# Two stages of a one-core transformer kernel: own buffers for the first slots behind the experts, another order of sums there, and other PSUM banks in block 1

## The reference

```python
# first block
proj = rms_norm(x, norm_mix) @ w_in             # qa ka va | qd kd vd | gates
out_na = neighbourhood_attention(qa, ka, va)    # 8 heads of 64
out_dil = dilated attention, 3 groups of 4 heads, softmax over all three groups
merged = sigmoid(gate_na) * (out_na @ w_branch_na) + sigmoid(gate_dil) * (out_dil @ w_branch_dil)
x = x + merged @ w_out
x = x + peer_ffn(rms_norm(x, norm_ffn))         # 16384 experts, 8 heads, top 16 each
h = rms_norm(x, norm_ple)
x = x + sigmoid(h @ w_ple_gate) * (p @ w_ple)
# second block: attention, pooling, feed forward, final norm
```

## Time and profile before

| | |
|---|---|
| time, median of 3 runs | 1334.89 us (1333.16 to 1335.21) |
| time of the profiled execution | 1334.01 us |
| its span, first to last instruction | 1331.8 us |
| TensorE busy | 1307.1 us (98%) |
| VectorE busy | 1018.5 us (76%) |
| ScalarE busy | 827.0 us (62%) |
| GpSimd busy | 513.2 us (39%) |
| mean granted TensorE clock | 0.994 of full speed |

### The profile page before, as it was taken

The page is one execution under the profiler, slowest core; times in us unless marked ns, Lnnn a source line. Parts: engine busy times, 40 slices in busy tenths (PEclk is TensorE's granted clock), DMA queues, the critical chain, the costliest instruction groups (busy, mean ns, idle before and its releaser), DMA issues.

```text
span 1331.8 us, 24822 instructions
## 1 busy us (share of the span) xinstructions
PE 1307.1 (98%) x9818; PEld 1261.1 (95%) x9818; DVE 1018.5 (76%) x1849; ACT 827.0 (62%) x1679; POOL 513.2 (39%) x248
## 2 busy tenths in 40 slices
PE   9999899999999999999999999999998999999997
PEld 9999799999999999999989999999998999999997
DVE  4573545759999888899978798998867855899943
ACT  6563556545455888888755565555565766666652
POOL 4745566578901000000024444434201553794442
PEclk9999999999999999999999999999998999999999
DMA  8433345555656555545569999999863544556552
GB/s 307 143 111 111 112 130 185 166 174 175 193 189 202 194 173 161 170 162 173 160 236 327 355 340 335 331 337 324 291 210 124 175 130 140 181 172 193 186 188 96
DMA packets 74299, 268.36 MB, mean 201 GB/s; under 512 B 8252, under 2 KB 8636, under 8 KB 74184
## 3 DMA queue, kind: packets, MB, share of 16 engines
q1 hardware_dynamic: 64968, 233.22, 52.7%
q0 software_dynamic: 9216, 33.56, 6.8%
HBM read 265.70 MB, written 1.05 MB: 200 GB/s over the span
## 4 chain that ended last, share of the span: by engine, by line
PE 81%; DVE 10%; POOL 3%; ACT 2%; DMA 1%; issue 1%; SPq 0%; DVEq 0%; ACTq 0%
PE PS L601 81%; POOL SPL L2242 1%; ACT SPL L1077 1%; DVE SPL L1520 1%; POOL HF L2301 1%; DMA RAW<-in_ev 1%; DVE ixu L1810 1%; DVE Ssc L1804 1%; DVE ixu L1801 1%; DVE bias L1599 0%; DVE top L1807 0%; DVE top L1798 0%; DMA RAW<-in_dense 0%; DVE HF L1537 0%; POOL HF L2299 0%
## 5 line engine op out<-in xcount | busy, mean ns | idle before, releaser
L1077 ACT ACTIVATE SPL<-RAW 128x1024 fp32r<-128x1024 f32 x432 | 456.9, 1059 | 373.3 <-PE PS L601 352.9
L601 PE MATMUL PS<-HS,SPL 128*128 128x224 f32 (+2 forms) x4016 | 540.9, 294 | 5.8 <-DVE SPL L1520 4.0
L601 PEld LDWEIGHTS PS<-HS,SPL 128*128 128x128 f32 x4016 | 511.4, 191 | 17.6 <-DVE SPL L1520 6.9
L2242 POOL TENSOR_TENSOR SPL<-RAW,SPL 128x1024 fp32r<-128x1024 f32 x148 | 359.6, 2434 | 335.3 <-ACT SPL L1077 335.1
L1520 DVE TENSOR_TENSOR SPL<-RAW,SPL 128x1024 fp32r<-128x1024 f32 x284 | 350.0, 1234 | 148.1 <-ACT SPL L1077 145.8
L601 PE MATMUL PS<-asp,SPL 128*128 128x448 f32 (+1 forms) x2048 | 322.1, 320 | 2.2 <-DVE GB L1920 1.2
L601 PEld LDWEIGHTS PS<-asp,SPL 128*128 128x128 f32 x2048 | 307.7, 190 | 16.1 <-DVE GB L1920 1.7
L2272 POOL DMA_INDIRECT rows<-in_er,RS x16 | 27.9, 1745 | 282.5 <-PE PS L601 250.1
L601 PE MATMUL PS<-HXb,SPL 128*128 128x256 f32 x720 | 89.3, 284 | 0.7 <-issue 0.6
L601 PEld LDWEIGHTS PS<-HXb,SPL 128*128 128x128 f32 x720 | 87.4, 189 | 1.3 <-issue 1.0
L1290 ACT ACTIVATE oh<-oh,T3f 128x128 f32<-128x128 f32 x224 | 71.4, 404 | 0.0
(11 more groups left out here) (286 smaller groups left out, 1498.4 us busy)
## 6 DMA issues: line engine op xcount, KB each, us to landing
RAW<-in_dense SPq DMA_DIRECT2D x176, 512.0 KB, 3.5
RAW<-in_eu SPq DMA_DIRECT2D x128, 512.0 KB, 3.5
RAW<-in_ev SPq DMA_DIRECT2D x128, 512.0 KB, 6.0
bias<-in_nab SPq DMA_DIRECT2D x2, 768.0 KB, 8.1
XT<-in_xT SPq DMA_DIRECT2D x4, 256.0 KB, 5.6
out_y<-HF SPq DMA_DIRECT2D x4, 256.0 KB, 2.2
c<-in_c SPq DMA_DIRECT2D x1, 960.0 KB, 9.1
c<-in_c SPq DMA_DIRECT2D x1, 512.0 KB, 4.9
```

What stands on the lines that cost most here:

```text
L601: return e.matmul(out, l, r, start=start, stop=stop, skip_group_check=skip)
L1077: e.activation(spl(n)[0], raw(n), ACT.Copy).then_inc(*up("act_high", ("hi", n)))
L2242: e.tensor_tensor(lo, raw(n), hi.bitcast(f32), ALU.subtract).then_inc(*up("pool_low", ("lo", n)))
```

## The change

At the end of the experts:

- Slots 333, 334 and 335 (`BEHIND`) get split buffers of their own: two in the space of `mixT`, one in a new region behind it, all inside the gates' storage that is free once value slot 80 has been prepared. Their high parts wait for that and no longer for the use of slots 330 to 332. Slots 336 to 338 take the ring buffers of slots 330 to 332 (`owner`).
- The low parts of slots 333, 334, 335 and 337 go from VectorE to GpSimd.
- The last pair's banks are finished in the order 7, 0, 1, 2, 3, 4, 5, 6 (`LAST_SUMS`).
- VectorE takes sum and low part of x in turn, and sums of squares from the sixth bank on. ScalarE cuts slots 333 and 334 ahead of its parts of x, slot 335 behind two of them, takes its squares from the fifth chunk on, and cuts 336 to 338 behind them.
- `norm_total(2)` comes behind the whole first pair of `pg`, not inside it.

In block 1: `bna` gets a ring of its own (banks 0, 1, 2), `dtr` takes bank 6 in place of 3, and the scores `dsc` 0, 1 and 2 come one place later, behind `vd` 4, `vd` 5 and `bna` 0.

```diff
+BEHIND = range(AFTER + 1, AFTER + 4)
+CLEARED = 80
+LAST_SUMS = (7, 0, 1, 2, 3, 4, 5, 6)
+def owner(n):
+    if n in BEHIND:
+        return None
+    return n - NSPL - (len(BEHIND) if AFTER + 4 <= n < AFTER + 4 + NSPL else 0)
 def low_on_dve(n):
-    if EXPERT + LISTED <= n < AFTER + 4:
+    if EXPERT + LISTED <= n <= AFTER:
         return True
...
-        return n in (AFTER + 5, *(SLOT0["w_in2"] + 2 * NE + i for i in (1, 2, 3, 4)))
+        return n in [SLOT0["w_in2"] + 2 * NE + i for i in (1, 2, 3, 4)]
...
-                ("dsc", 0), ("vd", 4), ("dsc", 1), ("vd", 5), ("dsc", 2), ("bna", 0), ("bna", 1), ("dex", 0), ("bna", 2),
+                ("vd", 4), ("dsc", 0), ("vd", 5), ("dsc", 1), ("bna", 0), ("dsc", 2), ("bna", 1), ("dex", 0), ("bna", 2),
...
+        ad = Arena()
+        late_split = ad.take("late_split", 2048, f32r)
+        ad.close()
+        behind = (mixTt[:, 0:2048], mixTt[:, 2048:4096], late_split)
         def spl(n):
+            if n in BEHIND:
+                b = behind[n - AFTER - 1]
+                return b[:, 0:1024], b[:, 1024:2048]
...
-        RINGS = {"lin": (0, 1), "lin1": (0, 1, 2), "scr1": (3, 4, 5), "pv": (6,), "dtr": (2, 7, 3), "dsc": (4, 5, 3),
-                 "va": (2, 6, 0, 1), "vd": (2, 0, 1, 6, 2, 6), "gn": (0, 1, 2, 6),
+        RINGS = {"lin": (0, 1), "lin1": (0, 1, 2), "scr1": (3, 4, 5), "pv": (6,), "dtr": (2, 7, 6), "dsc": (4, 5, 3),
+                 "va": (2, 6, 0, 1), "vd": (2, 0, 1, 6, 2, 6), "gn": (0, 1, 2, 6), "bna": (0, 1, 2),
...
-                    for c in (0, 1, 4, 5, 7, 6, 2, 3) if i == 0 else range(8):
+                    for c in (0, 1, 4, 5, 7, 6, 2, 3) if i == 0 else LAST_SUMS if i == NE - 1 else range(8):
...
-            run(linear("pg", 8, 8, rhs_x(2), x_of(2), "pg", pair=True, mid={6: lambda: norm_total(2)}))
+            gp = linear("pg", 8, 8, rhs_x(2), x_of(2), "pg", pair=True)
+            next(gp)
+            norm_total(2)
+            run(gp)
...
 # ScalarE, split(n)
-                if n >= NSPL:
-                    w.wait_ge(*at("used", n - NSPL))
+                if n in BEHIND:
+                    w.wait_ge(*at("apart", CLEARED))
+                elif n >= NSPL:
+                    w.wait_ge(*at("used", owner(n)))
...
 # ScalarE, end of the experts
-            w.wait_ge(*at("used", EXPERT + NE - 1))
-            for c in range(4):
-                gained(2, c)
             split(AFTER + 1)
             split(AFTER + 2)
-            for c in range(4, 8):
+            w.wait_ge(*at("used", EXPERT + NE - 1))
+            for n, c in enumerate(LAST_SUMS):
+                if n == 2:
+                    split(AFTER + 3)
                 gained(2, c)
-            fl = walk(cur, 8, 2, split, nothing)
-            for c in range(8):
-                next(fl)
-                if c >= 3:
-                    square(2, c - 3)
-            for c in range(5, 8):
-                square(2, c)
-            run(fl)
+                if n == 5:
+                    w.wait_ge(*at("used", AFTER - 1))
+                if n >= 5:
+                    square(2, 2 * n - 10)
+                    square(2, 2 * n - 9)
+            square(2, 6)
+            square(2, 7)
+            split(AFTER + 4)
+            split(AFTER + 5)
+            split(AFTER + 6)
...
 # VectorE, end of the experts
-            for c in range(4):
+            for n, c in enumerate(LAST_SUMS):
                 expert_sum(c)
-            split(AFTER + 1)
-            gained(2, 0)
-            for c in range(4, 8):
-                expert_sum(c)
-            gained(2, 1)
-            split(AFTER + 2)
-            gained(2, 2)
-            split(AFTER + 3)
-            for c in range(3, 8):
-                gained(2, c)
-            for c in range(8):
+                if n:
+                    gained(2, LAST_SUMS[n - 1])
+                if n > 5:
+                    sum_up(2, n - 6)
+            gained(2, LAST_SUMS[7])
+            for c in range(2, 8):
                 sum_up(2, c)
-            split(AFTER + 4)
```

More of the change, by code:

```diff
@@ L405, in build @@
         v2 = ar.take("v2", 1024).rearrange("p (a n) -> p a n", a=2)
-        mixT = ar.take("mixT", 4096, f32r).rearrange("p (s c t) -> p s c t", s=2, c=8)
+        mixTt = ar.take("mixT", 4096, f32r)
+        mixT = mixTt.rearrange("p (s c t) -> p s c t", s=2, c=8)
+        ad = Arena()
+        late_split = ad.take("late_split", 2048, f32r)
+        ad.close()
         dT = ar.take("dT", 1024).rearrange("p (c t) -> p c t", c=4)
@@ L703, in pe_program @@
                    "qkd": linear("qkd", 12, 8, rhs_x(0), x_of(0), "lin1"),
-                   "bna": linear("bna", 8, 4, lambda kk: (ona[:, 0, kk, :], ona[:, 1, kk, :]), lambda kk: ("ev", "na", kk)),
+                   "bna": linear("bna", 8, 4, lambda kk: (ona[:, 0, kk, :], ona[:, 1, kk, :]), lambda kk: ("ev", "na", kk), "bna"),
                    "gd": linear("gd", 8, 8, rhs_x(0), x_of(0)),
@@ L925, in pe_program @@
                         if i == NE - 1:
-                            t.then_inc(*up("pe_expert", ("vsum", c), *[("used", cur[0]), ("used", cur[0] - 1), ("v", i)] * (c == 7)))
+                            t.then_inc(*up("pe_expert", ("vsum", c), *[("used", cur[0]), ("used", cur[0] - 1), ("v", i)] * (c == LAST_SUMS[-1])))
                     if i < NE - 1:
@@ L1355, in act_program @@
                         weighed(i + 1)
-            w.wait_ge(*at("used", EXPERT + NE - 1))
-            for c in range(4):
-                gained(2, c)
             split(AFTER + 1)
             split(AFTER + 2)
-            for c in range(4, 8):
+            w.wait_ge(*at("used", EXPERT + NE - 1))
+            for n, c in enumerate(LAST_SUMS):
+                if n == 2:
+                    split(AFTER + 3)
                 gained(2, c)
-            fl = walk(cur, 8, 2, split, nothing)
-            for c in range(8):
-                next(fl)
-                if c >= 3:
-                    square(2, c - 3)
-            for c in range(5, 8):
-                square(2, c)
-            run(fl)
+                if n == 5:
[8 more added lines that the diff above has]
+            split(AFTER + 6)
+            cur[0] += 2
+            cur[1] += 16
             def pgate(n):
@@ L1383, in act_program @@
             warm(ACT.Sigmoid)
-            run(walk(cur, 8, 8, split, pgate, pair=True))
+            run(walk(cur, 8, 8, lambda n: split(n) if n > AFTER + 6 else None, pgate, pair=True))
             pgate(8)
```

## The result

The changed kernel takes 1321.01 us (median of 4 runs, 1320.71 to 1322.05), the kernel before 1334.39 us in the same comparison (4 runs, 1333.16 to 1335.21): ratio 0.9902, 95% interval 0.9885 to 0.9919, or 13.4 us less. All times and ratios here leave out two slow executions, both from the last group of the experiments: one of 1589.71 us at a mean granted clock of 0.75, and one of 4520.94 us of the kernel before.

What follows compares the result with a forecast made beforehand. The prediction took TensorE's matmul stream and its few stops to bound the kernel. Gains of 5.9 (expert end) and 4.4 (block 1), 10.3 us, took 1334.01 to 1323.7, on the median's scale 1324.6 us; range 1321.5 to 1329.5.

Steps and rivals of the forecast that it cites:

- Block 1: Three TensorE stops for bank reuse between 144 and 159 us go: 4.4 us gained, bounds 2.9 and 5.9.
- Expert end: From ple's start to pg's end, 30.7 us in place of 36.6: 5.9 us gained, bounds 3.5 and 7.1.
- rival 1: Expert end: VectorE gets no turn between GpSimd's three subtractions; 1326.9 us, or 1330.3 if the clock falls; chance 0.12.
- wait for the bank: Expert end: TensorE's first pg pair waits 0.3 us for VectorE's sum 5.
- wait for the sum of squares: Expert end: after the first pg pair TensorE waits 0.4 us for the sum of squares, semaphore included.
- norm and slot 336 together: Expert end: 0.34 us for the norm and 0.5 us of waiting for slot 336's low part.
- the pair: Expert end: the first pg pair, 48 matmuls, takes TensorE 5.84 us.
- the 144 matmuls: Expert end: the pg matmuls behind the first pair and the norm take 144/156 x 18.97 = 17.51 us.
- All that follows either stage hangs on TensorE, so the gain should reach the end.: Behind both edited stages: the whole 10.3 us gain should show in the kernel's time.
- The scale term: Whole kernel: the profiled execution lay 0.9 us under the median 1334.89, so 1323.7 became 1324.6 us.
- rival 2: Block 1: the clock's fall at 124 us, behind the twelve small matmuls, goes too; 1323.1 us, chance 0.15.
- Rivals 3, 4 and 5: Block 1 only moves stops: 1329.0, 0.07; later stage returns the gain: 1334.9, 0.04; clock stays 1.2 GHz: 1353.8, 0.04.

Runs made afterwards that it cites:

- e5: The kernel before with block 1's new bank rings for bna and dtr alone, order of steps as before: 1328.05 us, 0.9957.
- e4: The changed kernel with the low parts of slots 333, 334, 335 and 337 left on VectorE (337's unintentionally done twice): 1324.89 us, 0.9934.
- e2: The kernel before with block 1's edits alone, both rings and order of scores: 1328.79 us, 0.9967.
- e16: The kernel before with twelve more instructions on VectorE that clear a small tile early in the program: 1332.72 us, 0.9992.
- e3: The changed kernel with block 1 as before, so the expert end's edits alone: 1324.81 us, 0.9933.
- e7: The changed kernel with the last pair's banks in the order 0 to 7 again, sums of squares behind all sums: 1322.56 us, 0.9913.
- e15: The same program as e6 once more, on the chip of e14: 1319.79 us, 0.9898.
- e6: The changed kernel with all eight bank sums on VectorE ahead of the low parts of x: 1321.15 us, 0.9912.
- e1: The changed kernel once more, unchanged: 1319.99 us, 0.9900.
- e14: The changed kernel once more, unchanged, in a later comparison: 1321.87 us, 0.9909.
- e13: The kernel before with eight more instructions on GpSimd that clear a small tile early in the program: 1333.54 us, 0.9997.

## Why the prediction was too careful

**Block 1: right.** 4.4 us forecast, 4.38 and 4.37 us measured at equal clock. That the walk through the queues made the new order of the scores harmless is right as well; that the order is also useless (e5) the prediction didn't see.

**Expert end: mechanism right, sum 0.6 us too small.** 30.7 us forecast, 30.15 measured. VectorE was held 3.0 us as worked out and got a turn between the subtractions, so rival 1 is out. That adds with one operand in PSUM are not held was right too, but the two adds of the earlier trace rows (1009.69 and 1010.45) lie ahead of GpSimd's subtraction and don't show it; the changed kernel's do. By terms: wait for the bank 0.3, measured 0.49; wait for the sum of squares 0.4, measured 0; norm and slot 336 together 0.84, measured 0.85; the pair 5.84, measured 5.73; the 144 matmuls 17.51, measured 17.20. The prediction credits part of this to taking four low parts off VectorE. By e4 that is worth nothing up to the norm; what counted there, as far as the traces tell, is that the slots no longer wait for used buffers.

**The reading of the stop was wrong, though the sum was not.** I took the 3.31 us stop and the slow clock behind it for what made the stage long. e2 and e5 had a shorter fall and the same stage (36.65 us). Both were covered: the norm came 17.3 us behind ple's start in every kernel with the old order, whatever TensorE did. The new stage was added up from its own terms, so the error did not reach the forecast.

**The step that failed: "All that follows either stage hangs on TensorE, so the gain should reach the end."** The sum had no term for the program's last stretch, which is no matmul work. It became 1.0 us shorter (9.25 to 8.21), and an instruction packet 1.75 us ahead of the end went with it; e16 took both away without any other edit. Sum of the stages: 4.4 + 6.5 + 1.0 = 11.9, where the prediction had 10.3.

**The scale term was mis-sized, and was the largest part of the miss.** I added 0.9 us, since the profiled execution lay that far under a median of three runs. After the change the profiled execution lay 1.0 us above the median instead. The later medians of before were 1333.1 to 1334.0, below or at that profiled time, and the changed kernel's own three medians were 1321.01, 1319.99 and 1321.87. So 3.6 us = 1.0 (end of the program) + 0.6 (waits and matmul rate) + 1.9 (0.9 one way, 1.0 the other), within rounding. The last fits the scatter between sets of executions, whose parts are not all known: the clock's fall in block 1 alone (1.5 us) was there in twelve of the seventeen traces that keep the small matmuls together and absent in five (e2, e3, e7, e15, e16). The low end 1321.5 took in rival 2 and smaller waits, but nothing for the scale and nothing for the program's end.

**The rivals.** Rival 2, the clock's fall goes: the fall is no property of the order, since e6's program had it once (e6) and lost it once (e15); its 1.5 us belong to the scatter. It was there in all three traces of the changed kernel (37.43 to 37.46 us). Rivals 3, 4 and 5 are out: no stop moved, the gain reached the end, the clock was at 1.00 behind the wait of 0.49 us and across that of 0.25.

**Open.** The medians of the first two comparisons give 13.4 us, the stages 11.9. The intervals of e1 and e14 hold both figures, and no single stage was found for the difference.

## What to carry to other kernels

Price a stage by its own chain of events from a common start, not by the stops in it: here a stop of 3.31 us and a clock fall that cost TensorE up to 2.7 us (36 matmuls in 7.15 us, at the full clock 4.43) were both covered by VectorE's sums. When work moves to GpSimd, put those VectorE instructions that it holds behind GpSimd's run, not among it (with the sums first, 1.0 us here, e6). And when a gain of a few microseconds is to be forecast or explained, give the program's end and the scatter between sets of executions a term each; padding with idle instructions can tell an effect of the code's position from one of the change.

## What the runs showed of the hardware

- VectorE's scale-and-subtract with both operands in SBUF waits for a running GpSimd subtraction but gets in between two that follow each other: 0.64, 1.88 and 1.88 us in place of 0.48, and GpSimd's own took 2.48 to 2.60 us in place of 2.36. The waiting is the rule of the Trainium skill, page "SBUF — State Buffer", section "Who interferes with whom": a VectorE instruction with two inputs in SBUF and a GpSimd one that reads SBUF exclude each other. The turn between two instructions is what the traces add.
- The same program, executed again, may or may not have its clock fall behind the same small matmuls: 37.43 and 35.93 us for one stretch (e6, e15). In the expert end the same 36 matmuls behind the 3.31 us stop took 7.15 us in the kernel before, 5.80 in e2, 6.00 in e5 and, at the full clock, 4.43 in e16. The fall cost nothing where VectorE's sums covered it, and 1.0 to 1.2 us in e16, where it came behind the norm.
- Where an instruction packet comes with the last of the output stores (it starts 1.75 us ahead of the end), the tail is about 1.0 us longer: 9.25 to 9.73 us in six traces, 8.18 to 8.54 in fourteen without it. Twelve more VectorE instructions far ahead removed both (e16); eight on GpSimd did not (e13, 9.34 us).
